# Attention on one core: transposes in pairs in every second slot, query products and broadcasts in the odd slots

## The reference

```python
def attend(q_nope, q_rope, k_nope, k_rope, v):
    s = (jnp.einsum("bqhd,bkhd->bhqk", q_nope, k_nope)
         + jnp.einsum("bqhr,bkr->bhqk", q_rope, k_rope))
    p = jax.nn.softmax(s.astype(jnp.float32) * ATTN_SCALE, axis=-1).astype(v.dtype)
    return jnp.einsum("bhqk,bkhd->bqhd", p, v)
...
q = (rmsnorm(h @ w_dq, q_norm) @ w_uq).reshape(b, n, N_HEADS, QK_NOPE + QK_ROPE)
kv_a = h @ w_dkv
kv = (rmsnorm(kv_a[..., :KV_LORA], kv_norm) @ w_ukv).reshape(b, n, N_HEADS, QK_NOPE + V_HEAD)
```

## Time and profile before

| what | value |
|---|---|
| median of 3 runs | 2332.99 us (2331.04 to 2333.38) |
| profiled execution | 2330.7 us, span of its instructions 2329.4 us |
| PE busy | 2304.8 us, 99% of the span |
| DVE busy | 1698.0 us, 73% |
| ACT busy | 803.9 us, 35% |
| GpSimd busy | 118.7 us, 5% |
| granted TensorE clock | full speed in nearly all slices |

### The profile page before, as it was taken

One profiled execution on the slowest core, in us unless ns is written; L12 is line 12 of the kernel. 1 busy time (PEld: TensorE's weight loads), 2 busy tenths in 40 slices (PEclk: granted clock), 3 DMA queues, 4 the chain that ended last, 5 costly groups with the idle time before them and its releaser, 6 DMA issues.

```text
span 2329.4 us, 29137 instructions
## 1 busy us (share of the span) xinstructions
PE 2304.8 (99%) x10989; PEld 1907.7 (82%) x10989; DVE 1698.0 (73%) x2552; ACT 803.9 (35%) x1293; POOL 118.7 (5%) x90
## 2 busy tenths in 40 slices
PE   8999999999999999999999999999999999999998
PEld 5888888888888888888888788888888888888887
DVE  5777887886598888888886764264897777777777
ACT  6355555552443222222223411111532222222224
POOL 0101101000300000000001200001200000000002
PEclk9999999999999999999999999999999999999999
DMA  7101111132112333333322021121011111111112
GB/s 300 35 27 52 52 43 43 43 129 93 42 37 73 109 109 109 109 109 109 109 91 91 19 73 37 36 73 36 37 51 50 55 46 46 54 49 51 55 37 90
DMA packets 51960, 163.36 MB, mean 70 GB/s; under 512 B 7552, under 2 KB 12032, under 8 KB 51712
## 3 DMA queue, kind: packets, MB, share of 16 engines
q1 hardware_dynamic: 51840, 161.72, 20.7%
HBM read 157.51 MB, written 4.19 MB: 69 GB/s over the span
## 4 chain that ended last, share of the span: by engine, by line
PE 94%; DVE 4%; DMA 1%; ACT 1%; issue 0%; SPq 0%; POOL 0%; DVEq 0%; POOLq 0%; ACTq 0%
PE ps L635 26%; PE ps L637 26%; PE ps L636 26%; PE ps L1132 3%; PE ps L1066 2%; PE ps L1070 1%; PE ps L1068 1%; PE ps L1067 1%; PE ps L1071 1%; PE ps L1111 1%; PE ps L1113 1%; PE ps L1112 1%; DMA ada_ring<-ada_pe 1%; PE ps L902 1%; PE ps L911 0%
## 5 line engine op out<-in xcount | busy, mean ns | idle before, releaser
L2248 DVE SCALAR_TENSOR_TENSOR x<-ps,mods,x 128x512 f32<-128x512 f32 x440 | 322.7, 749 | 146.0 <-PE ps L637 126.7
L635 PE MATMUL ps<-g_hi,w_hi 128*128 128x512 f32 (+1 forms) x848 | 327.5, 386 | 0.1
L637 PE MATMUL ps<-g_hi,w_lo 128*128 128x512 f32 (+1 forms) x848 | 326.5, 385 | 0.0
L636 PE MATMUL ps<-g_lo,w_hi 128*128 128x512 f32 (+1 forms) x848 | 326.5, 385 | 0.0
L635 PE MATMUL ps<-h_hi,op_hi 128*128 128x512 f32 x640 | 249.2, 389 | 0.0
L637 PE MATMUL ps<-h_hi,op_lo 128*128 128x512 f32 x640 | 249.0, 389 | 0.0
L1779 ACT CAST op_hi<-rq 128x512 fp32r<-128x512 f32 x240 | 147.2, 623 | 234.1 <-PE ps L637 228.9
L1790 ACT ACTIVATE g_full<-g_full 128x512 f32<-128x512 f32 x80 | 50.8, 634 | 490.8 <-DVE g_full L2601 490.8
L635 PE MATMUL ps<-h_hi,w_hi 128*128 128x512 f32 x512 | 200.6, 392 | 1.6 <-DVE h_lo L2479 1.5
L637 PE MATMUL ps<-h_hi,w_lo 128*128 128x512 f32 x512 | 199.3, 389 | 0.0
L636 PE MATMUL ps<-h_lo,w_hi 128*128 128x512 f32 x512 | 199.3, 389 | 0.0
(11 more groups left out here) (365 smaller groups left out, 4492.0 us busy)
## 6 DMA issues: line engine op xcount, KB each, us to landing
rq<-stream SPq DMA_DIRECT2D x80, 512.0 KB, 3.6
mod_raw_f<-ada_rows SPq DMA_DIRECT2D x48, 512.0 KB, 3.5
raw<-stream SPq DMA_DIRECT2D x46, 512.0 KB, 3.6
w_lo_f<-stream SPq DMA_DIRECT2D x46, 512.0 KB, 4.4
mod_raw<-ada_rows SPq DMA_DIRECT2D x32, 512.0 KB, 3.5
ada_ring<-ada_pe SPq DMA_DIRECT2D x16, 512.0 KB, 11.3
x<-x_t SPq DMA_DIRECT2D x8, 512.0 KB, 7.3
x0a<-x_t SPq DMA_DIRECT2D x2, 1024.0 KB, 6.2
```

Of the source, the lines that this page charges most:

```text
L635: nc.tensor.matmul(out, w[0][wi], a[0][ai], start=start, stop=False)
L636: nc.tensor.matmul(out, w[0][wi], a[1][ai], start=False, stop=False)
L637: return nc.tensor.matmul(out, w[1][wi], a[0][ai], start=False, stop=stop)
L2248: nc.vector.scalar_tensor_tensor(out=x[:, m, HALF[half]], in0=ps[:, out_bank(d, m), :], scalar=mods[:, gate + m:gate + m + 1], in1=x[:, m, ...
```

## The change

`group_script` puts out the transposes of two key blocks in each even slot and none in the odd ones: slot 0 has T2 and T3, slot 2 T4 and T5, slot 4 T6 and T7, slot 6 T8 and T9, slot 8 T0 and T1 of the next group (called T10 and T11 below). B goes to slot 5. The query stage goes to odd slots: in `gb` 1 W and R0 in slot 3, R1 in 5, Q0 in 7, Q1 in 9; in `gb` 3 W in 3, Q0 in 7, Q1 in 9. Within a slot the order stays: PV, T, X, S and M, then the rest. On DVE `value_split` follows right behind `value_latent` in every group. What is computed, the number of instructions, the banks, and all tiles stay.

```diff
-QUERY_STAGE = (("W", 0), ("R", 0), ("R", 1), ("Q", 0), ("Q", 1))
-FOLLOW_AT = {4: ("W", 0), 6: ("Q", 0), 8: ("Q", 1)}
+LEAD_AT = {3: (("W", 0), ("R", 0)), 5: (("R", 1),), 7: (("Q", 0),), 9: (("Q", 1),)}
+FOLLOW_AT = {3: (("W", 0),), 7: (("Q", 0),), 9: (("Q", 1),)}
...
-        group, at = (gb, k + 2) if k + 2 < KT else (gb + 1, k + 2 - KT)
-        if not (last and group > 3):
-            out.append(("T", group, at))
+        for n in (k + 2, k + 3) if k % 2 == 0 else ():
+            group, at = (gb, n) if n < KT else (gb + 1, n - KT)
+            if not (last and group > 3):
+                out.append(("T", group, at))
...
-        if k == 4:
+        if k == 5:
             out.append(("B", gb, 0))
...
-            if pair_leads(gb) and 4 <= k <= 8:
-                out.append((QUERY_STAGE[k - 4][0], gb, QUERY_STAGE[k - 4][1]))
-            if not pair_leads(gb) and k in FOLLOW_AT:
-                out.append((FOLLOW_AT[k][0], gb, FOLLOW_AT[k][1]))
+            for kind, half in (LEAD_AT if pair_leads(gb) else FOLLOW_AT).get(k, ()):
+                out.append((kind, gb, half))
...
             elif kind == "PV" and k == KT - 1:
                 value_latent()
+                value_split()
             elif kind in RING_KINDS:
                 ring_lo(kind, k, gb, head_parity(gb))
-                if kind == "T" and k == 1 and gb > 0:
-                    value_split()
...
-                if last_pass and (kind, gb, k) == ("PV", 3, KT - 1):
-                    value_split()
```

## The result

The changed kernel takes 2355.78 us (median, 2354.52 to 2356.64), the kernel before on the same chip 2333.18 us: a ratio of 1.010, interval 1.0089 to 1.0112. It is slower by 22.6 us. The profiled execution takes 2355.26 us, 24.6 more than the one of before.

What follows compares the result with a forecast made beforehand. It took PE, busy 99% of the span, as the bound. Costs of 6.0, 2.6, 9.6, 3.6 and 1.6, less 0.8 and 1.5, gave 21.1 us: 2351.8 profiled, 2354 as median, range 2343 to 2364.

Steps and rivals of the forecast that it cites:

- cost 1: Slot 2: the exponential stands behind two copies on ACT, so PE waits before the score part; 0.40 x 15 = 6.0 us.
- cost 2: Slots 7 and 8: T11 waits for the bank of Q0, 0.43 us six times, 2.6 us.
- cost 3: Slots 9 and 0: T3 waits for Q1's bank, also held by slot 9's exponential; 1.6 us six times, 9.6 us.
- cost 4: Slot 3: W's rest queues on DVE, so its bank comes late; 3 x 0.9 + 3 x 0.3 = 3.6 us.
- first group, T3: Once, in the first group: T3 needs a bank whose copy stands behind an exponential; 1.6 us.
- last pass: Paired transposes stand a slot earlier there, but the last exponential stands behind two copies; -0.8 us, bounds -1 and +0.5.
- pairing: PE saves some 20 to 30 ns over a slot with 80 blocks fewer; 0 to 2.8 us, taken as 1.5.
- (a): Rival: PE pays a real switch of 0.085 us behind each block; 80 fewer give 6.8 us, 2326, faster; 5%.
- (b): Rival: nothing moves, as new waits fall where PE would wait anyway or ACT's copies come earlier; 2333, 4%.
- (c): Rival: DVE at 80% doesn't recover from its backlog, and each of 15 groups loses 1.2 us more; 2372, 9%.
- (d): Rival: bunched transposes let the clock fall to 1.2 GHz in attention; up to some 2770 us, 1%.

Runs made afterwards that it cites:

- e3: The changed kernel with slot 2's exponential and row inverse placed between the copies of T4 and T5; 2352.04 us.
- e10: The changed kernel with e5's edit, and the value split and scaling on DVE also put behind Q1's rest; 2353.06 us.
- e5: The changed kernel with slot 9's exponential moved behind Q1's copy on ACT, in gb 1 and 3 only; 2355.01 us.
- e1: The changed kernel with B and the query stage back in their old slots, so only the transposes are paired; 2347.53 us.
- e2: The kernel before with only the query stage and B moved to the odd slots, transposes singly; 2340.84 us.
- e6: The changed kernel with the row inverse on DVE moved from slot 2 to slot 0; 2356.74 us.
- e9: As e7, but in the last pass the value split again stands behind the rest of the next group's second block; 2334.00 us.
- e4: The kernel before with the three PV matmuls placed inside the block of four transposes that follows them; 2339.18 us.
- e7: The changed kernel with pairs kept in the looped passes, single transposes in the last, and work reordered to take the waits out; 2335.86 us.
- e8: The changed kernel with DVE's modulation rows in attention cut from 1024 to 128 columns; 2355.76 us.

## Why the prediction was right

Forecast 2354 (2343 to 2364) and slower, measured 2355.78. Point by point, by starts:

| step | forecast | measured |
|---|---|---|
| exponential of slot 2 (cost 1) | 0.40 x 15 = 6.0 | 12 of 0.436 to 0.460, 3 in the last pass of 0.36 to 0.39: 6.4; and 0.25 once, at the exponential of slot 4 |
| T11 behind Q0 (cost 2) | 0.43 x 6 = 2.6 | 0.439 to 0.448 x 6 = 2.6 |
| T3 behind Q1 (cost 3) | 1.6 x 6 = 9.6 | 1.643 to 1.657 x 6 = 9.9 |
| W (cost 4) | 0.9 x 3 + 0.3 x 3 = 3.6 | 0.80 x 3 + 0.12 x 3 = 2.8 |
| first group, T3 | 1.6 | 1.56 |
| last pass | -0.8 | 1.65 for 2.4 before = -0.7 |
| restart behind a wait | none | tails 3.0, and 0.2 in two gaps of over 0.09 us, which are among the waits: 3.2 |
| pairing | -1.5 | 78 changes of kind: -0.2; small -2.1, not by the pairing |
| sum | 21.1 | 23.8 in attention |

- **Cost 1** held in every number: 0.96 from copy to exponential (0.98 forecast), 1.48 on to the score part, 0.43 late. e3 takes it out. The 15 that I counted are there; the three in the last pass are smaller, for a reason that wasn't tested. The waits view names pbuf 16 times on PE's weight loads: the sixteenth is the exponential of slot 4, once in the last pass (513.00), which waits for a row maximum and not for two copies. My sum hadn't got it.
- **Costs 2 and 3** held within 0.06 us a time. e10 shows the direct price of cost 3, e5 and e10 the two queues that lie over it, and e1 and e2 that it needs both halves of the change. I took 1.6 and not 1.1 because DVE's maximum can't move; the timeline above bears that out.
- **Cost 4** was mis-sized by 0.8 in all, and not on DVE's side. From the copy of T4 to the release of W's bank the prediction has 5.72 (429.98 to 435.7) and the changed kernel 5.74 in gb 3, with DVE busy all the way. PE came later than forecast: from the late score part to T7 I had 2.34, and it is 2.49, of which 0.11 is the restart behind the exponential. In gb 1 the allowance of 0.3 was an estimate without a sum, and 0.12 was measured. Taking the inverse away gains only 0.3 (e6), since the maximum then waits for its scores.
- **The restart** was missing. A matmul that waits has its weight load waiting too, and the lead has to be made again: 0.11 us behind each of 16 exponentials, 0.056 behind each of 22 waiting transposes, a few more in the last pass.
- **The pairing's saving** had the size but not the cause. I put 1.5 us on 80 blocks fewer, at 20 to 30 ns a slot. e9 has pairs in all looped passes and small stands at 7.2, before at 6.9; e4 has blocks cut in two and small doesn't move. Small goes with how often PE waits: 6.9 to 7.2 with 5 to 16 waits (before, e4, e7, e9), 6.3 with 24 (e2, which has no pairs), 5.8 with 27 (e3), 5.3 with 40 (e1), 4.8 with 42 (the changed kernel). Why it does wasn't tested. That this saving came near my 1.5 is luck.

In attention the sum is 2.7 short: 3.2 for the restarts and 1.1 in costs 1 to 3 and the places that come once, less 0.85 for cost 4 and 0.8 for small and pairing. The profiled executions differ by 24.6 us and the medians by 22.6, so that the median came within 1.8 us is partly luck.

**The rivals.** (a), a real switch: no, by e4 and e9. (b), nothing moves: no, PE has no slack to take waits up, each one is in the time. (c), backlog: no, by e8. (d), the clock: the granted clock is 1.00 in the row of 130 to 573 us, which is the full level, with 78 runs of eight transposes in it. The Trainium skill, TensorE: Matmul & The Clock Gate, Part 4 (PE-mode transpose), has transposes not counted as busy in the way of matmuls. The lower clock that (d) took from it did not come: the granted clock stayed full with eight in a row in every second slot. Whether transposes count can't be told here, since there are matmuls between all the blocks.

## What to carry to other kernels

When one engine is busy 99% of the time and a ring of two banks ties it to the others, what an item costs is set by how much of the bounding engine's work lies between it and the item two before: count that in start gaps, against the chain last start, copy, rest, release. Putting like work together takes that work away just where it was the cover, and gains nothing unless a trace shows that the change of kind costs something. In an engine's queue ask what stands directly ahead of the piece that releases, not how full the engine is.

## What the runs showed of the hardware

- A matmul released by a semaphore starts together with its weight load instead of one matmul behind it. The matmul after it comes 0.107 to 0.11 us later than its usual gap (16 of 16 behind the exponential, 256 columns); behind a waiting transpose it is 0.055 to 0.06.
- Changing between fp32 transposes and fp32r matmuls costs about 3 ns (e4), and eight transposes in a row keep the spacing of 0.109 us of four: 1.03 to 1.04 us for eight.
- The idle time of the waits view is less than the lateness of the waiting instruction, since ends of overlapped matmuls are modelled: 0.28 for 0.43, 1.48 for 1.65, 0.64 for 0.80. PE's weight loads overstate it by the lead that they have (0.71 for 0.43). Forecast and measurement agreed to 0.06 us, in costs 1 to 3, only once both were taken from starts.
